# Expert blocks in column quarters, with tokens turned on VectorE and a one-hot token table

## The reference

```
logits = hf @ w_router + b_router;  top_v, top_e = top_k(logits, 4);  gates = softmax(top_v)
gu   = xb @ w_gu + b_gu                      # 1024 -> 2048, per expert
gate = min(gu[:, :1024], 7);  up = clip(gu[:, 1024:], -7, 7)
y    = ((up + 1) * gate * sigmoid(1.702 * gate)) @ w_dn + b_dn      # 1024 -> 1024
out  = sum over a token's four experts of y * gate weight
```

## Time and profile before

| | us |
|---|---|
| median of 3 runs (1816.2 to 1819.22) | 1817.5 |
| the profiled execution | 1819.62 |
| its span | 1817.8 |

### The profile page before, as it was taken

How to read it: one execution, slowest core, us unless ns; L and a number is a source line. 1 busy time by engine, 2 the same in 40 slices (tenths; PEclk the granted TensorE clock), 3 DMA queues, 4 the chain that set the end, 5 groups by cost and what they waited for, 6 DMA issues and landing times.

```text
span 1817.8 us, 39267 instructions
## 1 busy us (share of the span) xinstructions
PE 1570.0 (86%) x16465; PEld 750.6 (41%) x16465; DVE 701.1 (39%) x1414; ACT 323.9 (18%) x678; POOL 155.7 (9%) x241
## 2 busy tenths in 40 slices
PE   3998888789992299999999999999999999999920
PEld 2664754555652044344443433433433433433400
DVE  1379996433346022232222222222222222222248
ACT  2231116333321011111111111111111111111001
POOL 1024104000111300000000000000000000000031
PEclk8898998655995599999999999999999999999965
DMA  9235548000444579999999999999999999997763
GB/s 346 77 106 186 186 172 300 1 4 3 151 177 156 205 310 408 402 407 401 408 406 399 396 400 390 392 403 393 391 402 392 388 409 391 393 402 272 306 249 109
DMA packets 129291, 531.20 MB, mean 292 GB/s; under 512 B 12634, under 2 KB 22156, under 8 KB 95444
## 3 DMA queue, kind: packets, MB, share of 16 engines
q1 hardware_dynamic: 100112, 472.07, 66.4%
q0 software_dynamic: 12272, 41.28, 6.9%
q10 hardware_dynamic: 16852, 17.11, 2.8%
HBM read 501.04 MB, written 29.37 MB: 292 GB/s over the span
## 4 chain that ended last, share of the span: by engine, by line
PE 50%; DMA 36%; DVE 6%; ACT 3%; issue 2%; POOL 1%; ACTq 1%; SPq 0%; DVEq 0%; POOLq 0%
DMA down_w<-in_w_down 32%; PE psum L1712 9%; PE psum L1694 8%; PE psum L1720 6%; PE psum L1515 5%; PE psum L1703 4%; PE psum L1653 3%; PE psum L1619 2%; PE psum L1523 2%; PE psum L1634 2%; DMA front_ring<-in_w_in 1%; DVE final_work L1277 1%; PE psum L1494 1%; PE psum L1627 1%; POOL slot_dram L1420 1%
## 5 line engine op out<-in xcount | busy, mean ns | idle before, releaser
L1712 PE MATMUL psum<-down_w,expert_work 128*32 128x512 f32 x2112 | 240.0, 595 | 17.2 <-DMA down_w<-in_w_down 17.2
L1694 PE MATMUL psum<-gu_even,expert_work 128*32 128x512 f32 x2176 | 239.1, 597 | 1.3 <-ACT expert_work L824 1.0
L1215 DVE TENSOR_TENSOR expert_work<-psum,expert_work 128x512 f32<-128x512 f32 x66 | 36.8, 558 | 500.6 <-PE psum L1694 372.1
L1694 PE MATMUL psum<-gu_odd,expert_work 128*32 128x512 f32 x2048 | 222.7, 592 | 0.0
L1233 DVE TENSOR_TENSOR expert_work<-psum,expert_work 128x512 f32<-128x512 f32 x66 | 36.9, 558 | 303.0 <-PE psum L1712 214.9
L1694 PEld LDWEIGHTS psum<-gu_even,expert_work 128*32 128x32 f32 x2176 | 70.9, 111 | 159.4 <-issue 156.8
L1712 PEld LDWEIGHTS psum<-down_w,expert_work 128*32 128x32 f32 x2112 | 63.0, 109 | 155.2 <-issue 120.1
L1694 PEld LDWEIGHTS psum<-gu_odd,expert_work 128*32 128x32 f32 x2048 | 66.6, 110 | 146.3 <-issue 143.6
L1703 PE MATMUL psum<-gu_even,expert_work 128*32 128x256 f32 x2176 | 124.0, 380 | 0.0
L1720 PE MATMUL psum<-down_w,expert_work 128*32 128x256 f32 x2112 | 120.0, 379 | 0.0
L1703 PE MATMUL psum<-gu_odd,expert_work 128*32 128x256 f32 x2048 | 116.8, 380 | 0.0
(11 more groups left out here) (308 smaller groups left out, 1616.9 us busy)
## 6 DMA issues: line engine op xcount, KB each, us to landing
gu_even<-in_w_gate_up SPq DMA_DIRECT2D x68, 2048.0 KB, 22.7
down_w<-in_w_down SPq DMA_DIRECT2D x66, 2048.0 KB, 23.3
gu_odd<-in_w_gate_up SPq DMA_DIRECT2D x64, 2048.0 KB, 22.9
front_ring<-in_w_mod SPq DMA_DIRECT2D x12, 2048.0 KB
ys_dram<-raw_ring POOLq DMA_DIRECT2D x1, 8448.0 KB, 39.3
ys_dram<-expert_work ACTq DMA_DIRECT2D x66, 128.0 KB, 7.2
front_ring<-in_w_in SPq DMA_DIRECT2D x4, 2048.0 KB
front_ring<-in_w_mod_final SPq DMA_DIRECT2D x4, 2048.0 KB
```

Of the source, the lines that this page charges most:

```text
L1215: v.tensor_tensor(eg[part], psum[:, 2 * part, 0:w], bias_of(bias_b, part, 0), ALU.add).then_inc(gu_added, 1)
L1694: last = mm(psum[32 * u:32 * u + 32, x, :], lhsT=xgT[:, k, 32 * g_:32 * g_ + 32], rhs=gu_slot(par, c)[:, k % 2, at_:at_ + WA], start=(k == ...
L1712: last = mm(psum[32 * u:32 * u + 32, 4, :], lhsT=actT[0][:, at_:at_ + 32], rhs=dn_slot(c)[:, k % 4, n * WA:(n + 1) * WA], start=(k == 0), ...
```

## The change

- Tokens of a block are three groups of GT = 32. Gate-up and down are computed per group in four column quarters of 256, one per strip of the array.
- Each group's rows are gathered as 128 pieces of 1 KB (32 tokens x 4 quarters, one quarter per strip), three indirect DMAs a block. A DVE transpose of 32x32 pieces then gives xgT directly. The activations are transposed on DVE too. PE and ACT do none in the blocks. xgT has two buffers.
- Weight rows are laid out with row index 8p + k on partition p, so that a gate-up chunk is one run of 16 KB per partition (at a pitch of 64 KB), and so is a down chunk (at 32 KB). Bias rows are two DMAs of four partitions, and the shuffle has 768 columns.
- ys rows of a group leave in one DMA of 128 pieces of 1 KB, three a block.
- The token table is computed: one-hot rows times one-hot groups, summed over the 20 columns on PE (step "table"), instead of stored and loaded. The overflow list comes by a PE transpose (step "over").
- Overflow blocks have 32 slots (NOV = 57) and run one group.
- SP issues expert 1's gate-up weights after step ("hT", 4) and the stores of x2 and h, ahead of the bias rows.
- ACT loads the sigmoid table once before the loop.

```diff
-ROWS_B = 96
-NOV = 22
+GT, GB = 32, 3
+ROWS_B = GT * GB
+NOV = 57
+NG = GB * NE + NOV
+TABW = NG + GB
-    s += [("rank",)]
+    s += [("rank",), ("table",), ("over",)]
...
-        w_gu = a["w_gate_up"][0].rearrange("e (k p) n -> e p k n", p=P)
-        w_dn = a["w_down"][0].rearrange("e (k p) n -> e p k n", p=P)
+        w_gu = a["w_gate_up"][0].rearrange("e (p k) n -> e p k n", p=P)
+        w_dn = a["w_down"][0].rearrange("e (p k) n -> e p k n", p=P)
...
             def bias_rows(e):
+                at_ = slice(0, P, GT)
+                sp.dma_start(brow[at_, 0:2 * QW].rearrange("u (t n) -> u t n", t=2),
+                             a["b_gate_up"][0][bass.ds(e, 1), :].rearrange("e (t u n) -> (e u) t n", t=2, u=QUARTERS)).then_inc(bias_in, 16)
+                sp.dma_start(brow[at_, 2 * QW:3 * QW],
+                             a["b_down"][0][bass.ds(e, 1), :].rearrange("e (u n) -> (e u) n", u=QUARTERS)).then_inc(bias_in, 16)
...
-            sp.wait_ge(routed, 1)
+            filled(sp, JOB[("hT", T - 1)])
             for x, y in ((x2_stored[0], 3), (x2_stored[1], 2), (h2_stored[0], 3), (h2_stored[1], 2)):
                 sp.wait_ge(x, 16 * y)
+            for c in range(GUC):
+                load_gu(1, c, 1)
             sp.wait_ge(brow_clear, 1)
             bias_rows(0)
-            for c in range(GUC):
-                load_gu(1, c, 1)
...
+            def store_rows(n, g_):
+                act_e.wait_ge(ys_ready, n + GB + 1)
+                act_e.dma_start(ys_dram[bass.ds(n * GT, GT), :].rearrange("t (u n) -> u t n", u=QUARTERS),
+                                ysb[g_]).then_inc(ys_stored, 16)
...
+                    for tt in range(T):
+                        cols = slice(TOPE * tt, TOPE * (tt + 1))
+                        v.tensor_tensor(at_group[:, cols, :], iota_g.unsqueeze(1).to_broadcast([P, TOPE, NG]),
+                                        f6[:, cols].unsqueeze(2).to_broadcast([P, TOPE, NG]), ALU.is_equal)
+                        for c in range(TOPE * tt, TOPE * (tt + 1)):
+                            ins = v.tensor_scalar(at_row[:, c, :], iota_r, f3[:, c:c + 1], tok4[:, tt:tt + 1], ALU.is_equal, ALU.mult)
+                        ins.then_inc(hot_made, 1)
...
+            def turn_tokens(b, par):
+                dve.wait_ge(gathered, (b + 1) * (GB * 16))
+                dve.sem_inc(turn_settled, 1)
+                v.transpose(xgT[par].rearrange("p g k n -> p (g k) n"),
+                            xg.rearrange("p (g f k) -> p g k f", g=GB, k=KD)).then_inc(xgT_ready, 1)
+
+            def gated(n, g_):
+                gate, up = gu_s[g_][:, 0:QW], gu_s[g_][:, QW:2 * QW]
+                v.tensor_tensor(halves(gu_s[g_]), psum[:, 2 * g_:2 * g_ + 2, 0:QW], halves(bias_b[:, 0:2 * QW]), ALU.add).then_inc(gu_added, 1)
...
+                v.transpose(actT[g_], up.rearrange("p (f k) -> p k f", k=KD)).then_inc(actT_ready, 1)
...
+            def expert_dve(b, par):
+                turn_tokens(b + 1, 1 - par)
+                dve.wait_ge(bias_ready, b + 1)
+                for g_ in range(GB):
...
+                    gated(b * GB + g_, g_)
+                dve.wait_ge(ys_stored, (b + 1) * (GB * 16))
+                for g_ in range(GB):
...
+                    rows_out(b * GB + g_, g_)
+                spread_bias(b + 1, (b + 1) * GB)
...
-            pool.wait_ge(routed, 1)
-            pool.wait_ge(tab_zero, 16)
-            n = 0
-            for t in range(T):
-                for k in range(TOPE):
-                    c = 4 * t + k
-                    g.indirect_dma_start(slot_dram, bass.IndirectOffsetOnAxis(tab_pos[0:ROWS[t], c:c + 1], 0),
-                                         tok_id[0:ROWS[t], t:t + 1], None).then_inc(tab_written, 16)
-                    n += 1
...
+                for g_ in range(n):
+                    g.indirect_dma_start(xg[:, g_ * QW:(g_ + 1) * QW], None, h_quarters,
+                                         bass.IndirectOffsetOnAxis(idx_now[:, g_:g_ + 1], 0)).then_inc(gathered, 16)
...
+                elif kind == "table":
+                    for tt in range(T):
+                        pe.wait_ge(hot_made, tt + 1)
+                        rws = ROWS[tt]
+                        for c in range(TOPE * tt, TOPE * (tt + 1)):
+                            last = mm(bank(j)[:, 0:NG], lhsT=at_row[0:rws, c, :], rhs=at_group[0:rws, c, :],
+                                      start=(c == 0), stop=(c == T * TOPE - 1))
...
+            def gate_up(g_, par, c, xT):
                 for k in (2 * c, 2 * c + 1):
                     for x in range(2):
+                        for u in range(QUARTERS):
+                            last = mm(psum[GT * u:GT * u + GT, 2 * g_ + x, 0:QW], lhsT=xT[:, g_, k, :],
+                                      rhs=gu_slot(par, c)[:, k % 2, x * D + u * QW:x * D + (u + 1) * QW],
+                                      start=(k == 0), stop=(k == KD - 1))
+                return last
...
+            def down(g_, c):
                 for k in range(4 * c, 4 * c + 4):
+                    for u in range(QUARTERS):
+                        last = mm(down_sum(g_)[GT * u:GT * u + GT, :], lhsT=actT[g_][:, k, :],
+                                  rhs=dn_slot(c)[:, k % 4, u * QW:(u + 1) * QW], start=(k == 0), stop=(k == KD - 1))
                 return last
...
+            def expert_pe(b, par, use_gu, groups, n):
+                for g_ in range(groups):
+                    for c in range(GUC):
+                        if g_ == 0:
+                            pe.wait_ge(gu_in[par][c], use_gu * 16 + 16)
+                        last = gate_up(g_, par, c, xgT[par])
+                        if g_ == groups - 1:
+                            last.then_inc(gu_done, 1)
...
+                for g_ in range(groups):
+                    pe.wait_ge(actT_ready, n + g_ + 1)
+                    if g_ != 1:
+                        pe.wait_ge(ys_ready, n + GB + g_ // 2)
+                    for c in range(DNC):
+                        if g_ == 0:
+                            pe.wait_ge(dn_in[c], b * 16 + 16)
+                        last = down(g_, c)
...
```

More of the change, by code:

```diff
@@ L304, in build @@
         oneh = op.take(T * TOPE * NE)
+        at_group = op.ap[:, op.at - T * TOPE * NE:op.at - T * TOPE * NE + T * TOPE * NG].rearrange("p (c n) -> p c n", n=NG)
+        op.take(T * TOPE * (NG - NE))
         rank = op.take(T * NE + NE)
-        tmpn = op.take(NOV * NE)
-        iota_j = op.take(NOV * NE)
-        xb_, xe_, xst = op.take(NE), op.take(NE), op.take(NE)
+        iota_g, iota_r = op.take(NG), op.take(P)
+        xb_, xe_, xst, x31 = op.take(NE), op.take(NE), op.take(NE), op.take(NE)
         rj = op.take(NE)
         pick_t = op.take(T * TOPE * NE)
+        at_row = op.ap[:, op.at - T * TOPE * NE:op.at + T * TOPE * (P - NE)].rearrange("p (c n) -> p c n", n=P)
+        op.take(T * TOPE * (P - NE))
         sel_before = op.take((T + 1) * NE)
         ex = Carver(ex_t, EX_WORDS)
[L314 to L326, removed]
+        xg = ex.take(GB * QW)
+        xgT = [ex.take(KD * ROWS_B).rearrange("p (g k n) -> p g k n", g=GB, k=KD) for _ in range(2)]
+        gu_s = [ex.take(2 * QW) for _ in range(GB)]
+        es = [ex.take(QW) for _ in range(GB)]
+        actT = [ex.take(QW).rearrange("p (k n) -> p k n", k=KD) for _ in range(GB)]
+        ysb = [ex.take(QW) for _ in range(GB)]
+        brow, bias_b = ex.take(3 * QW), ex.take(3 * QW)
         fi = Carver(fin_t, FIN_WORDS)
@@ L1252, in _ @@
             v.memset(brow, 0.0).then_inc(brow_clear, 1)
[L1253 to L1256 removed]
+            dve.sem_inc(ys_ready, GB)
+            turn_tokens(0, 0)
+            spread_bias(0, 0)
+            with dve.Fori(0, NE // 2) as p_:
+                expert_dve(p_ * 2, 0)
+                expert_dve(p_ * 2 + 1, 1)
+            in_sbuf(dve, ("over",))
             n_over = dve.value_load(over[0:1, NOV:NOV + 1], min_val=0, max_val=NOV)
@@ L1698, in gate_up_rest @@
-            def gate_up_rest(par, c):
+                elif kind == "table":
+                    for tt in range(T):
[4 more added lines that the diff above has]
+                                      start=(c == 0), stop=(c == T * TOPE - 1))
+                elif kind == "over":
+                    pe.wait_ge(routed, 1)
+                    last = tr(bank(j)[0:1, 0:P], ocol, ident)
@@ L1744, in _ @@
+            in_sbuf(pe, ("over",))
             in_sbuf(pe, ("rt", T - 1))
-            turn_tokens(0)
             with pe.Fori(0, NE // 2) as p_:
-                expert_pe(p_ * 2, 0, p_)
-                expert_pe(p_ * 2 + 1, 1, p_)
-            pe.wait_ge(routed, 1)
+                for par in range(2):
+                    pe.wait_ge(xgT_ready, p_ * 2 + par + 1)
+                    expert_pe(p_ * 2 + par, par, p_, GB, p_ * (2 * GB) + par * GB)
+            in_sbuf(pe, ("over",))
             n_over = pe.value_load(over[0:1, NOV:NOV + 1], min_val=0, max_val=NOV)
```

324 lines of the change are left out of this document (120 added, 204 removed).

## The result

The changed kernel takes 2052.2 us (median of four runs, 2049.7 to 2058.6) against 1818.4 for the kernel before on the same chip (four runs): a ratio of 1.129, 95% interval 1.126 to 1.132. The forecast was 1755, with 0.08 on slower. 234 us were added where 62 were to go.

A forecast was written before the change was run, and what follows sets the result against it. Bound: DMA weight loads in the expert stage, TensorE's limit close by. Of 62 us saved, 24 come from routing, 16 overflow, 1.5 block 31's PE, 21 the stage: 1755 us against 1817.5, range 1718 to 1802.

The forecast's parts named there:

- The step that failed: Output stores in the expert blocks: they have until the next block's first row copy; no landing time was given.
- The DMA part: Transfers in a block: bytes stay, bias falls from 1.05 to 0.35 us, small pieces add 0.35, 16 KB rows save 0.4.
- Routing: Stretch before the experts: computed token table brings the first expert matmul to 603.0 from 626.66 us, 23.7 us removed.
- PE in a block: Expert block on TensorE: 576 matmuls of 256 columns, no transposes, floor falls from 32.84 to 31.5 us.
- VectorE in a block: Gating, row copies, shuffle and token transpose in an expert block: 12 to 18 us of 33, under TensorE's time.
- DMA period: Expert stage: a block takes 32.9 + 0.35 + 0.35 - 0.4 = 33.2 us, above TensorE's floor, against 33.97 before.
- The lone engine: Expert stage: one DMA engine of 16 ends late, 1.05 us a block, because of small bias packets; falls to 0.35.
- Rival 1: Expert stage: the lone engine stays late, 432 gather packets a block, period stays 33.97 us, 1778 us in all; 20%.
- Overflow: The one overflow block after the experts: a single group, 17.1 us instead of 33.4.
- The tail: Final gathers and norm after the overflow block: untouched, 80.4 us.
- Rival 2: Expert stage: DMA drops out as the bound, period 32.2 us or below, 1725 down to 1711 us in all; 17%.
- Rival 3: Expert stage: strided 16 KB weight rows are slower, 1791 to 1842 us; 18%, half of it beyond 1817.

The follow-up runs named there:

- a_wide: The changed kernel with each group's store cut into four DMAs of 32 rows by 256 columns, on all sixteen engines: 1808.8 us, 0.995 of before.
- a_wide_unroll: The changed kernel with stores on sixteen engines and TensorE's 32 blocks written out as straight code: 1731.9 us, ratio 0.9515 to before.
- b_rows16: The kernel before with its weights in 16 KB rows and nothing else of the change: 1806.2 us, ratio 0.992 to 0.996.
- b_bias2: The kernel before without its four two-partition bias loads per expert, the two four-partition ones kept: 1795.1 us, ratio 0.985 to 0.989.
- the pair of a_wide_unroll kernels: The changed kernel with sixteen-engine stores and straight TensorE code, with 16 KB weight rows (1731.9 us) and with the old 8 and 4 KB rows (1749.8 us).
- a_twobuf: The changed kernel with two sets of output row buffers by block parity, stores left on four engines: 1812.3 us.
- b_narrow: The kernel before with its six stores a block made into two, going to two and four engines: 1972.5 us, 153 us slower.

## Why the prediction was wrong

**The step that failed** is one sentence in the part on VectorE: "Stores of a block have until the next block's first row copy." It names the right deadline and gives the store no landing time. The deadline was to be had: 21 us of gate-up and 3.5 of the first down group, 25 us. So was a bound on the landing. The sentence before it counts the gather at 27 packets an engine, each behind a 16 KB packet at 0.62 us. The same sum for the stores is 96 pieces, since the count of four is outermost: 96 x 0.62 = 60 us, over 25 and so no longer hidden (measured: 41, of which TensorE stood 14 idle). For the bias the prediction did count the engines by the outermost dimension; it did not do so for the store, whose address pattern the change rewrote. With the store mended (a_wide) 243 us go, more than the 234 lost. The DMA part priced the stores' 1 KB pieces by bytes over sixteen engines, +0.35 us, which prices their share of the traffic and not their landing.

**A term that was missing.** The floor of 31.5 us counted 576 matmuls a block, more than before, but only their time. That they and their weight loads no longer fit where a loop body is kept (2304 instructions for two blocks) wasn't weighed. It cost 77 to 111 us. That the stage before had no packets on queue 8 was there to be seen; what a larger body would do, no row of before showed.

**With both taken out, the other steps can be read**, in a_wide_unroll, 1731.9 against the forecast 1755:
- *Routing.* First expert matmul 600.59 (604.53 in the changed kernel, whose front ran some 4 us later from before the sums on), forecast 603.0, before 626.66. The sum is right, in part by luck, since its terms were off both ways: the table is bound by VectorE and not by TensorE's 10.6 us (a pair of its matmuls took about 0.33 us, not 0.53) and is done at 591.5 instead of 593.7, the gather lands in 2.7 and not in 4.2, and the transpose of 128x768 costs 1.55, not 0.95.
```profile
600.59 22.66 PE psum L1688 x384
```
- *PE in a block.* 20.72 + 10.41 = 31.13 us at full clock (the free block of a_wide), 54.0 and 54.2 ns a matmul, against 31.5. Right; the weight loads do stay under the matmuls.
- *VectorE in a block.* 38.61 us in 100, 12.5 a block: within 12 to 18, and under PE.
- *DMA period.* 33.2 forecast, 32.36 measured. The 16 KB rows were put at -0.4 and came out at -0.55 here and -0.39 in b_rows16. The bias loads were to save 1.05 - 0.35 = 0.70, and b_bias2 saved 0.77. What failed is the +0.35 for small pieces: with the old rows the changed kernel (its stores mended) has 32.91, and b_bias2, with as many bias loads but the old gather and stores, has 33.20. So the new ones cost nothing. For the gather the term had no ground: in the trace a block's three gathers are 144 packets, not 432, and 96 of them have 4 KB, as before. Totals of 592 to 599.5 us, which hold those gathers and 20 packets of bias:
```profile
DMA packets 164, 0.41 MB, mean 54 GB/s; under 512 B 56, under 2 KB 68, under 8 KB 164
```
- *The lone engine.* Its cause, inferred from small packets, holds: b_bias2. Rival 1 falls with it, since the changed kernel has two bias loads a block and, with its stores mended, no such wait; the 432 packets that spoke for it are 144.
- *Overflow.* 17.1 forecast, 21.7 measured (1631.29 to 1652.95). The chain there:
```profile
1631.29 0.43 DVE expert_work L1218
...
1634.25 8.84 PE psum L1688 x128
...
1646.49 6.43 PE psum L1696 x64
1652.95 0.44 DVE expert_work L1218
```
  The gaps of 3 us are as forecast. The matmuls take 15.3 instead of 10.9, since the clock falls in those gaps (granted 0.81 over 1634 to 1643, 0.57 over 1646 to 1653).
- *The tail.* 1732.6 - 1652.95 = 79.7 against 80.4.
- *Rival 2*, DMA dropping out as the bound, nearly holds: its condition was a P of 32.2 or below, and 32.36 is 1.2 above the PE floor. With that P alone the forecast's sum gives 1755 - 30 x 0.84 = 1730; the 4.6 us that the overflow took more and the 2.4 that routing took less nearly cancel. *Rival 3*, slower weight rows, is refuted by b_rows16 and by the pair of a_wide_unroll kernels. None of the rivals was the mechanism that decided: the three with a chance were about the rate of the weight loads, and none about who waits for the transfer that the change reshaped. The sign "wrong if gate-up matmuls wait for xgT or for VectorE" did not show it either: it was the down matmuls that waited for VectorE.

## What to carry to other kernels

For each transfer that an edit reshapes, write down its outermost count, pieces for each engine, and the packets they take turns with, and compare that landing with the next reuse of its buffer; bytes over bandwidth says nothing about it. Sharing the store among sixteen engines and giving it a second set of buffers removed the same loss here (1808.8 and 1812.3 us). When an edit multiplies instructions in a loop, count matmuls and weight loads of the body together, and look for instruction-queue packets in the steady stage. In a loop they came with a gap at every jump here; in straight code they came without one.

## What the runs showed of the hardware that I had not expected

- Beside 16 KB packets of another queue, three stores of 128 1-KB pieces on four engines took 41 us to land, 0.42 us a piece of an engine; alone, one such store took 3.27 us. With 8 and 4 KB weight packets the same stores held nobody.
- A backward jump in a body of 2304 or 3184 instructions left TensorE idle 4.7 to 6.2 us, and its next matmuls then ran at a lower granted clock, 0.50 in their first 4 us (23.70 us for what takes 20.72; 16.22 for 13.92). Straight code for 32 blocks was fetched at a similar rate without idle time.
- Four loads of 8 or 4 KB to two partitions each cost a block 0.77 us of a stage that moves 13 MB in 34 us.
- Three indirect gathers of 384 rows of 1 KB in all moved as 96 packets of 4 KB, and landed no later than 96 rows of 4 KB.
- A narrow store pattern cost in two ways: in the changed kernel it held a buffer (a_twobuf hides it), in the kernel before it made TensorE wait for weights (b_narrow, +153 us). The two differ in packet size and in the count of engines too, so what decides between the ways is not shown.
